# A two-block transformer kernel on Trainium2: the first pair of columns behind each norm as three float32r products

## The chip, the cores and the metric

The kernel runs on one core of one Trainium2 chip. The metric is the device time of one execution in microseconds (us); the time before is 2511.12 us, the median of 3 runs (2510.36 to 2512.72).

The core has five engines that run side by side and wait for each other through semaphores: TensorE (PE: matmuls from SBUF into PSUM), VectorE (DVE), ScalarE (ACT), GpSimd (POOL, SBUF only) and SyncE (SP, which issues the transfers here). PEld is the weight load of TensorE.

## The reference, cut to what matters

Two blocks of a network with 512 tokens and 1024 channels. The second one, where six of the seven places of the change lie, runs twice:

```python
def second_block(x, norm_g, ffn_w_gate, ffn_w_up, ffn_w_down, w_in, conv_w, pool_w, pool_scale, w_out):
    for l in range(DEPTH_2):
        g = norm_g[l]
        f = _swiglu(_rmsnorm_2(x, g[0]), ffn_w_gate[l, 0], ffn_w_up[l, 0], ffn_w_down[l, 0])
        x = x + 0.5 * _rmsnorm_2(f, g[1])
        m = _mixer(_rmsnorm_2(x, g[2]), w_in[l], conv_w[l], pool_w[l], pool_scale[l], w_out[l])
        x = x + _rmsnorm_2(m, g[3])
        f = _swiglu(_rmsnorm_2(x, g[4]), ffn_w_gate[l, 1], ffn_w_up[l, 1], ffn_w_down[l, 1])
        x = x + 0.5 * _rmsnorm_2(f, g[5])
    return x
```

`_rmsnorm_2(x, g)` is x / sqrt(mean(x²) + 1e-6) · g over the 1024 channels; `_swiglu` is silu(h @ w_gate) · (h @ w_up) @ w_down with 2816 hidden channels; `_mixer` is a projection, a stick-breaking attention over 8 heads beside a short convolution and a pooling, and a projection w_out back to 1024. The first block ends in a feed-forward part too, w_up of 1024 x 4096 behind a modulated norm of x; this norm's place is called x1 here.

## The kernel before

**Layout.** Channels lie on the 128 partitions, tokens along the free dimension: x is 8 chunks (DC = 8) of 128 x 512. A matrix product makes one *unit* of 128 output channels: for each of the 8 (or 11, in the second half of a feed-forward part) chunks of input channels one 128x128 weight tile times a 128x512 chunk, summed in one PSUM bank.

**Split products.** Almost every product is made as three float32r matmuls (L581 to L583): high part of the weights times high part of the input, high times low, low times high. The high part is a copy to float32r; the low part is what is left, full minus high. For the weights ACT makes w_hi from the loaded tile raw (`refill`, L1056) and POOL makes w_lo = raw - w_hi (L492). Weights come in *pairs* p of slots s = 0 and 1; SP loads raw for a slot when POOL has taken its low part before (lo_ready), ACT refills a slot when TensorE is through with the unit that read it (unit_done), and a unit starts when its w_lo is there (lo_ready) and its PSUM bank is free (taken).

**The first pair behind a norm.** At seven places the input of the next product has only just been made: behind x1 (L1001 to L1010) and behind norm(0) to norm(5). There the first pair of output columns is made from the *unsplit* tensors, as one float32 matmul per chunk and column: first_raw (loaded by `load_first` long ahead, in the arena's slots 12 to 15) times u_all (or u1), 16 matmuls into the two score banks (L669, L1007). After chunk 6 stands `spread`, the transposed inverse root (L638).

**Norm r**, r = 0 to 6; the last has nothing behind it. It overlaps the 8 units of the projection that come before it, the *down* units. Behind norm(0) these have 8 chunks each, behind norm(1), (3), (4) and (6) they have 11, and behind norm(2) and norm(5), which close a mixer (w_out), 8. For each output chunk c of that projection:

- DVE takes it from PSUM into f (L1982 or L1986), from norm(1) on also makes the cross product x·g·f and adds it up (L1920, L1921), and adds the two squares that ACT made to their sums (L1931, L1915).
- ACT, in this order and per slot: `refill` of the slot that the unit has freed, then f_sq and gf_sq (L1073, L1075) once DVE has taken the chunk.

Then come TensorE's token sums (L630) between thin matmuls that only keep the array busy (`keep_warm`, L625), ACT's root, DVE's reciprocal, TensorE's spread; then the update phase: DVE makes the new x chunk by chunk (L2003, L2005; in norm(0) L1989), ACT makes u_all from x (L1097) and u_hi from u_all (L1100), TensorE the first products, and when all of x is there DVE makes the 8 low parts u_lo (L1971). TensorE then goes on with the pair p+1 from u_hi and u_lo. The weights of its slot 0 are refilled between f_squares of chunk 6 and 7, those of slot 1 after chunk 1 of the update phase.

No table sets an order: each engine runs its instructions in the order written.

## Time and profile before

| | |
|---|---|
| median of 3 runs | 2511.12 us (2510.36 to 2512.72) |
| profiled execution, its own time | 2510.76 us |
| its span, first to last instruction | 2509.0 us |
| granted TensorE clock, mean | 0.997 |
| PE busy | 2477.5 us (99%) |
| DVE busy | 1283.5 us (51%) |
| ACT busy | 908.2 us (36%) |
| POOL busy | 983.5 us (39%) |
| DMA | 253 MB, mean 101 GB/s |

A matmul's record is longer than the step to the next one, since matmuls are pipelined; a busy share of 99% says that TensorE is hardly ever without work, not what the work costs. A start-to-start step does.

### The profile page before, as it was taken

What the parts mean: (1) busy time and instruction counts of PE and PEld (TensorE: products, weight loads), DVE (VectorE), ACT (ScalarE), POOL (GpSimd) and SP (SyncE); (2) the same over time, 40 slices, a digit from 0 to 9 for tenths busy, and PEclk for the clock granted to TensorE, in tenths of its full rate; (3) what the DMA queues carried; (4) which work ended last, traced back from release to release, by engine and by line L of the source; (5) the groups of instructions that cost most, each with busy time, mean ns of one, the idle gap of its engine ahead of it and who ended that gap; (6) DMA issues with size and microseconds to landing.
All of it is one profiled execution on the core that took longest, in us unless ns stands there. A gap on an engine that the chain in (4) does not pass through costs nothing.

```text
span 2509.0 us, 32788 instructions
## 1 busy us (share of the span) xinstructions
PE 2477.5 (99%) x11384; PEld 1986.7 (79%) x11384; DVE 1283.5 (51%) x1780; ACT 908.2 (36%) x1295; POOL 983.5 (39%) x445
## 2 busy tenths in 40 slices
PE   7999999999999999999999999999999999999998
PEld 4878778887788887777788887788887777788886
DVE  6664767256431358678431348431358678431334
ACT  4444543234321234454431234321234454431231
POOL 4333424443344443333343443344443333343443
PEclk9999999999999999999999999999999999999998
DMA  6222644322233231322233232233231322232232
GB/s 237 90 81 86 222 163 134 109 97 88 75 104 105 93 107 60 94 83 93 75 102 108 92 105 80 75 105 104 93 107 60 95 82 92 75 102 91 92 104 80
DMA packets 72904, 253.39 MB, mean 101 GB/s; under 512 B 9056, under 2 KB 11232, under 8 KB 72704
## 3 DMA queue, kind: packets, MB, share of 16 engines
q1 hardware_dynamic: 72832, 252.46, 30.3%
q8 instruction: 42, 0.69, 0.1%
q14 instruction: 30, 0.25, 0.0%
HBM read 244.76 MB, written 2.10 MB: 98 GB/s over the span
## 4 chain that ended last, share of the span: by engine, by line
PE 87%; issue 9%; POOL 2%; DVE 1%; DMA 1%; SPq 0%; ACT 0%; POOLq 0%; DVEq 0%; ACTq 0%
PE unit_bank L581 26%; PE unit_bank L583 26%; PE unit_bank L582 26%; PE score L669 3%; POOL w_lo L492 2%; PE mix L725 1%; PE out_bank L705 1%; PE score L1007 1%; PE mix L625 1%; PE mix L733 0%; DMA ada_in_u<-in_w_ada 0%; PE out_bank L630 0%; PE mix L630 0%; PE stat_bank L638 0%; PE score L630 0%
## 5 line engine op out<-in xcount | busy, mean ns | idle before, releaser
L492 POOL TENSOR_TENSOR w_lo<-raw,w_hi 128x1024 fp32r<-128x1024 f32 (+2 forms) x374 | 954.6, 2552 | 1483.7 <-ACT w_hi L1056 1483.7
L1056 ACT ACTIVATE w_hi<-raw 128x1024 fp32r<-128x1024 f32 (+2 forms) x375 | 415.9, 1109 | 1199.3 <-PE unit_bank L583 1177.9
L581 PE MATMUL unit_bank<-u_hi,w_hi 128*128 128x512 f32 x2152 | 845.9, 393 | 0.5 <-POOL w_lo L492 0.5
L583 PE MATMUL unit_bank<-u_hi,w_lo 128*128 128x512 f32 x2152 | 837.8, 389 | 0.0
L582 PE MATMUL unit_bank<-u_lo,w_hi 128*128 128x512 f32 x2152 | 837.7, 389 | 0.0
L581 PEld LDWEIGHTS unit_bank<-u_hi,w_hi 128*128 128x128 f32 x2152 | 403.9, 188 | 101.7 <-issue 16.0
L583 PEld LDWEIGHTS unit_bank<-u_hi,w_lo 128*128 128x128 f32 x2152 | 404.0, 188 | 84.8
L582 PEld LDWEIGHTS unit_bank<-u_lo,w_hi 128*128 128x128 f32 x2152 | 404.1, 188 | 84.2 <-issue 1.9
L581 PE MATMUL unit_bank<-h_hi,w_hi 128*128 128x512 f32 x992 | 387.0, 390 | 0.2 <-DVE h_lo L1881 0.2
L583 PE MATMUL unit_bank<-h_hi,w_lo 128*128 128x512 f32 x992 | 385.9, 389 | 0.0
L582 PE MATMUL unit_bank<-h_lo,w_hi 128*128 128x512 f32 x992 | 385.9, 389 | 0.0
L2033 DVE TENSOR_TENSOR arena<-unit_bank,rstd 128x512 f32<-128x512 f32 x84 | 58.1, 692 | 398.9 <-PE unit_bank L583 398.9
L581 PEld LDWEIGHTS unit_bank<-h_hi,w_hi 128*128 128x128 f32 x992 | 186.2, 188 | 39.5 <-DVE h_lo L1881 0.7
L582 PEld LDWEIGHTS unit_bank<-h_lo,w_hi 128*128 128x128 f32 x992 | 186.2, 188 | 39.1 <-issue 0.5
L583 PEld LDWEIGHTS unit_bank<-h_hi,w_lo 128*128 128x128 f32 x992 | 186.2, 188 | 38.9
L2042 DVE TENSOR_TENSOR h_lo<-arena,h_hi 128x512 f32 (+1 forms) x88 | 167.8, 1906 | 81.6 <-ACT h_hi L1345 81.6
L1986 DVE COPY f<-unit_bank 128x512 f32 (+1 forms) x48 | 33.2, 691 | 211.6 <-PE unit_bank L583 205.1
L2030 DVE TENSOR_TENSOR arena<-unit_bank,rstd 128x512 f32<-128x512 f32 x84 | 58.1, 692 | 121.1 <-PE unit_bank L583 121.1
L669 PE MATMUL score<-arena 128*128 128x512 f32 x192 | 85.4, 597 | 0.1
L1921 DVE TENSOR_TENSOR arena<-arena 128x512 f32<-128x512 f32 x40 | 84.2, 2105 | 1.4
L1931 DVE TENSOR_TENSOR arena<-arena 128x512 f32<-128x512 f32 x49 | 59.6, 1216 | 17.8 <-ACT arena L1073 13.5
L669 PEld LDWEIGHTS score<-arena 128*128 128x128 f32 x192 | 35.0, 190 | 42.1 <-issue 34.5
(337 smaller groups left out, 1938.0 us busy)
## 6 DMA issues: line engine op xcount, KB each, us to landing
raw<-in_w_gate_up SPq DMA_DIRECT2D x168, 512.0 KB, 3.5
raw<-in_w_down SPq DMA_DIRECT2D x64, 704.0 KB, 4.1
...
```

The source lines that it names most:

```text
L492: e.tensor_tensor(w_lo[:, s, 0:n], raw[:, s, 0:n], as32(w_hi[:, s, 0:n]), ALU.subtract).then_inc(lo_ready, 1)
L581: e.matmul(bank[:], wh, hi(k), start=n == 0, stop=False)
L582: e.matmul(bank[:], wh, lo(k), start=False, stop=False)
L583: mm = e.matmul(bank[:], wl, hi(k), start=False, stop=last)
L669: mm = e.matmul(score[s][:], first_raw[:, s, c * P:(c + 1) * P], u_all[:, c, :], start=c == 0, stop=c == DC - 1)
L1056: e.activation(w_hi[:, s, 0:n], raw[:, s, 0:n], ACT.Copy).then_inc(hi_ready, 1)
L1921: step(e.tensor_tensor(cross_acc, cross_acc, cross, ALU.add))
L1931: step(e.tensor_tensor(f_acc, f_acc, f_sq, ALU.add))
L1986: e.tensor_copy(flat(f[:, bass.ds(c, 1), :]), unit_bank[s][:]).then_inc(taken[s], 1)
L2030: g = e.tensor_tensor(ffn_g, banks[0][:], rstd[:], ALU.mult)
L2033: u = e.tensor_tensor(ffn_u, banks[1][:], rstd[:], ALU.mult)
L2042: e.tensor_tensor(flat(h_lo[:, bass.ds(i, 1), :]), ffn_h, as32(flat(h_hi[:, bass.ds(i, 1), :])), ALU.subtract).then_inc(h_ready, 1)
```

## The change

At the seven places the first pair becomes a split product too. New are first_hi (ACT, `first_high`) and first_lo (POOL, `split_first`, over first_raw in place). `first_units` on TensorE makes, per chunk c, four matmuls from u_hi (first_hi and first_lo, two columns each) and, one chunk later, two from u_lo with first_hi: 48 float32r matmuls of 128x512 in place of 16 float32 ones.

Around it:

- ACT makes u_hi straight from x and then u_all from x; the refill of slot 1 of pair p+1 moves behind all eight chunks, that of slot 0 ahead of the squares of chunk 6; first_high stands ahead of chunk 4's refill and ahead of that of slot 0 of p+1; root_u is made after chunk 3 in place of 5, and lies in PSUM.
- POOL makes u_lo of chunks 0 to 5, DVE only those of 6 and 7.
- DVE's reciprocal inv_u stands after chunk 5 in place of 7; the copy into pool_w moves behind the norm's first takes in the mixer.
- At x1 the same order holds: ACT makes u_hi and u1 from ux, POOL six low parts, DVE two.
- TensorE has one more keep_warm ahead of the first products.

SP's program is the same. The core of the diff:

```diff
@@ -153,13 +154,16 @@
         sq, x_acc, ux = slots(0, 2), slot(2), slots(4, 2)

         f_sq, gf_sq, f_acc, cross, cross_acc, gf_acc = (slot(n) for n in range(6))
-        root_f, root_u, inv_f, inv_u, scaled = (slot(11)[:, 128 + 4 * n:132 + 4 * n] for n in range(5))
+        root_f, inv_f, inv_u, scaled = (slot(11)[:, 128 + 4 * n:132 + 4 * n] for n in range(4))
         x_sum = stat[:, 0:TB]
         root_x, inv_x = stat[:, 0:TB], stat[:, TB:2 * TB]
         u1 = slots(16, 8)
         u_all = slots(16, 8)
         first_raw = arena[:, 12 * T:16 * T].rearrange("p (s n) -> p s n", s=2)
         ffn_g, ffn_s, ffn_u, ffn_h = slot(6), slot(7), slot(8), slot(9)
+
+        first_hi = nc.alloc_sbuf_tensor_at("first_hi", [P, 2, D], F32R, offset=arena_at + 6 * T * 4)
+        first_lo = nc.alloc_sbuf_tensor_at("first_lo", [P, 2, D], F32R, offset=arena_at + 12 * T * 4)
         a_pad = arena[:, 10 * T:10 * T + T + 2]
         q_st, k_st, vT_st = slot(16), slot(17), slot(18)
         v_nat = slots(19, 1)[:, 0, :].rearrange("p (i d) -> p i d", d=P)
@@ -549,15 +558,44 @@
             e.tensor_tensor(w_lo[:, 1, 0:D], raw[:, 1, 0:D], as32(w_hi[:, 1, 0:D]), ALU.subtract).then_inc(lo_ready, 1)
             split_pairs(IN1 + 2, MERGE1 - IN1 - 2, D)
             split_pairs(MERGE1, DC // 2, 6 * P)
-            split_pairs(OUT1, LAYER0 - OUT1, D)
+            def split_first(q, s):
+
+                e.wait_ge(first_hi_ready, 2 * q + s + 1)
+                e.tensor_tensor(first_lo[:, s, :], first_raw[:, s, :], as32(first_hi[:, s, :]),
+                                ALU.subtract).then_inc(first_lo_ready, 1)
+
+            def split_next(q, last, n, p):
+
+
+                if q:
+                    split_first(q, 0)
+                split_pair(last, n)
+                if q == 0:
+                    split_first(q, 0)
+                split_first(q, 1)
+                split_one(p, 0, D)
+                for c in range(DC - 2):
+                    e.wait_ge(uhi_ready, DC * (1 + q) + c + 1)
+                    e.wait_ge(u_full, DC * q + c + 1)
+                    e.tensor_tensor(u_lo[:, c, :], u_all[:, c, :], as32(u_hi[:, c, :]),
+                                    ALU.subtract).then_inc(u_ready, 1)
+                split_one(p, 1, D)
+
+            split_pairs(OUT1, DC // 2 - 1, D)
+            split_next(0, FFN1, D, FFN1 + 1)
+            split_pairs(FFN1 + 2, LAYER0 - FFN1 - 3, D)
             for l in range(LAYERS):
                 for s in range(2):
                     for half in range(2):
-                        p0, skip = ffn2(l, s, half), 1 - half
+                        p0, skip = ffn2(l, s, half), 2 - 2 * half
+                        if half == 0:
+                            split_next(FIRST_OF_NORM + 3 * l + 2 * s, p0, D if s or l == 0 else RING, p0 + 1)
                         split_pairs(p0 + skip, HALF2 - skip, D)
-                        split_pairs(p0 + HALF2, DC // 2, RING)
+                        rest = half == 0 or (l == LAYERS - 1 and s == 1)
+                        split_pairs(p0 + HALF2, DC // 2 if rest else DC // 2 - 1, RING)
                     if s == 0:
-                        split_pairs(mix2(l) + 1, MIX2_PAIRS, D)
+                        split_next(FIRST_OF_NORM + 3 * l + 1, mix2(l), RING, mix2(l) + 1)
+                        split_pairs(mix2(l) + 2, MIX2_PAIRS - 2, D)
             for n, c in enumerate(POOL_SUMS):
                 e.wait_ge(f_scaled, n + 1)
                 e.tensor_tensor(x[:, c, :], f[:, c, :], x[:, c, :], ALU.add).then_inc(x_summed, 1)
@@ -639,6 +677,30 @@
                                   start=True, stop=True)
                 mm.then_inc(spread_ready, 1)

+            def first_units(q, at=None, insert=None):
+
+
+                def low(c):
+                    e.wait_ge(u_ready, DC * (1 + q) + c + 1)
+                    for s in range(2):
+                        mm = e.matmul(score[s][:], first_hi[:, s, c * P:(c + 1) * P], u_lo[:, c, :], start=False,
+                                      stop=c == DC - 1)
+                        if c == DC - 1:
+                            mm.then_inc(first_done, 1)
+
+                e.wait_ge(first_lo_ready, 2 * q + 2)
+                for c in EIGHT:
+                    e.wait_ge(uhi_ready, DC * (1 + q) + c + 1)
+                    for w in (first_hi, first_lo):
+                        for s in range(2):
+                            e.matmul(score[s][:], w[:, s, c * P:(c + 1) * P], u_hi[:, c, :],
+                                     start=c == 0 and w is first_hi, stop=False)
+                    if c:
+                        low(c - 1)
+                    if c == at:
+                        insert()
+                low(DC - 1)
+
             def norm(r):


@@ -660,18 +722,8 @@
                 if r:
                     mm = token_sums(cross_sum, cross_acc)
                 mm.then_inc(cross_sums, 1)
-                keep_warm(3)
-                for s in range(2):
-                    e.wait_ge(first_loaded[s], 16 * (FIRST_OF_NORM + r + 1))
-                for c in EIGHT:
-                    e.wait_ge(u_full, DC * r + c + 1)
-                    for s in range(2):
-                        mm = e.matmul(score[s][:], first_raw[:, s, c * P:(c + 1) * P], u_all[:, c, :],
-                                      start=c == 0, stop=c == DC - 1)
-                        if c == DC - 1:
-                            mm.then_inc(first_done, 1)
-                    if c == 6:
-                        spread(2 * r + 2, inv_u, mix[1])
+                keep_warm(4)
+                first_units(FIRST_OF_NORM + r, 6, lambda: spread(2 * r + 2, inv_u, mix[1]))

             def u_chunk(m):
                 return lambda c: e.wait_ge(u_ready, DC * (2 + m) + c + 1)
@@ -999,15 +1051,7 @@
                               start=True, stop=True)
             mm.then_inc(x1_spread, 1)
             keep_warm(6)
-            for s in range(2):
-                e.wait_ge(first_loaded[s], 16)
-            for c in EIGHT:
-                e.wait_ge(u1_full, c + 1)
-                for s in range(2):
-                    mm = e.matmul(score[s][:], first_raw[:, s, c * P:(c + 1) * P], u1[:, c, :], start=c == 0,
-                                  stop=c == DC - 1)
-                    if c == DC - 1:
-                        mm.then_inc(first_done, 1)
+            first_units(0)
             for half in range(2):
                 p0 = FFN1 + half * FFN1_HALF
                 if half == 0:
@@ -1074,19 +1118,31 @@
                 if g is not None:
                     e.activation(gf_sq, fc, ACT.Square, scale=g(c)).then_inc(fsq_ready, 1)

+            def first_high(q, s):
+
+                e.wait_ge(first_loaded[s], 16 * (q + 1))
+                e.activation(first_hi[:, s, :], first_raw[:, s, :], ACT.Copy).then_inc(first_hi_ready, 1)
+
             def norm(r, p, part, g):


                 ahead = r < NORMS - 1
                 g = g if ahead else None
-                with e.Fori(0, DC // 2 - 1) as i:
+                def pair(i):
                     for s in range(2):
                         refill(p + i + 1, s, D if r in (2, 5) or r == 0 else RING)
                         f_squares(p + i, s, part, 2 * i + s, g)
+
+                with e.Fori(0, DC // 2 - 2) as i:
+                    pair(i)
+                if ahead:
+                    first_high(FIRST_OF_NORM + r, 0)
+                pair(DC // 2 - 2)
                 p = p + DC // 2 - 1
+                if ahead:
+                    first_high(FIRST_OF_NORM + r, 1)
+                    refill(p + 1, 0)
                 f_squares(p, 0, part, DC - 2, g)
-                if ahead:
-                    refill(p + 1, 0)
                 f_squares(p, 1, part, DC - 1, g)
                 e.wait_ge(sums_ready, r + 1)
                 token_root(root_f, square_sum)
@@ -1094,15 +1150,13 @@
                     return
                 for c in range(DC):
                     e.wait_ge(x_ready, DC * r + c + 1)
-                    e.activation(u_all[:, c, :], x[:, c, :], ACT.Identity,
-                                 scale=col("norm_g", 2 * r * DC + c)).then_inc(u_full, 1)
-                    e.wait_ge(u_full, DC * r + c + 1)
-                    e.activation(u_hi[:, c, :], u_all[:, c, :], ACT.Copy).then_inc(uhi_ready, 1)
-                    if c == 1:
-                        refill(p + 1, 1)
-                    if c == 5:
+                    gain = col("norm_g", 2 * r * DC + c)
+                    e.activation(u_hi[:, c, :], x[:, c, :], ACT.Identity, scale=gain).then_inc(uhi_ready, 1)
+                    e.activation(u_all[:, c, :], x[:, c, :], ACT.Identity, scale=gain).then_inc(u_full, 1)
+                    if c == 3:
                         e.wait_ge(grown_ready, r + 1)
                         token_root(root_u, x_sum)
+                refill(p + 1, 1)
                 e.wait_ge(spread_ready, 2 * r + 2)
                 e.activation(rstd[:], mix[1][:], ACT.Copy).then_inc(rstd_ready, 1)

@@ -1265,6 +1319,9 @@
                     if c:
                         e.wait_ge(taken[(c - 1) % 2], p0 + (c - 1) // 2 + 2)
                         square(q, c - 1)
+                    if c == refills - 1:
+                        for s in range(2):
+                            first_high(0, s)
                     if c < refills:
                         refill(p0 + c // 2 + 1, c % 2)
                 e.wait_ge(taken[1], p0 + DC // 2 + 1)
@@ -1960,14 +2016,15 @@
                             e.tensor_tensor(x_sum, x_sum, grown, ALU.add).then_inc(grown_ready, 1)
                         else:
                             e.tensor_tensor(x_sum, scaled, inv_f, ALU.mult).then_inc(grown_ready, 1)
-                    if c == DC - 1 and ahead:
+                    if c == 5 and ahead:
                         e.wait_ge(root_ready, 2 * r + 2)
                         e.reciprocal(inv_u, root_u).then_inc(inverse_ready, 1)
                 if not ahead:
                     return
-                for c in range(DC):
-
-                    e.wait_ge(uhi_ready, DC * (2 + r) + c + 1)
+                e.wait_ge(u_ready, DC * (2 + r) + DC - 2)
+                for c in range(DC - 2, DC):
+
+                    e.wait_ge(u_full, DC * (1 + r) + c + 1)
                     e.tensor_tensor(u_lo[:, c, :], u_all[:, c, :], as32(u_hi[:, c, :]),
                                     ALU.subtract).then_inc(u_ready, 1)
                 e.wait_ge(rstd_ready, r + 1)
```

Norm(2), the place between the mixer's w_out and the feed-forward part, on POOL. w_lo, raw and w_hi are the weights' low part, full tile and high part, hi_ready ACT's word that w_hi is there. Before, one turn of the loop over pairs, which runs on through the norm:

```order
L492 TENSOR_TENSOR w_lo<-raw,w_hi 128x1024 [waits hi_ready]
L491 REGISTER_ALU
L492 TENSOR_TENSOR w_lo<-raw,w_hi 128x1024 [waits hi_ready]
L496 REGISTER_ALU
L496 COMPARE_AND_BRANCH
```

Now, from the end of that loop's turns on:

```order
L497 TENSOR_TENSOR w_lo<-raw,w_hi 128x1024 [waits hi_ready]
L505 REGISTER_ALU
L505 COMPARE_AND_BRANCH
L564 TENSOR_TENSOR first_lo<-arena,first_hi 128x1024 [waits first_hi_ready]
L497 TENSOR_TENSOR w_lo<-raw,w_hi 128x1024 [waits hi_ready] x2
L564 TENSOR_TENSOR first_lo<-arena,first_hi 128x1024 [waits first_hi_ready]
L497 TENSOR_TENSOR w_lo<-raw,w_hi 128x1024 [waits hi_ready]
L580 TENSOR_TENSOR u_lo<-arena,u_hi 128x512 [waits u_full,uhi_ready] x6
L497 TENSOR_TENSOR w_lo<-raw,w_hi 128x1024 [waits hi_ready]
```

Two splits of the first pair have come in around the splits for the last two down units, and six of u_lo stand between slot 0 and slot 1 of the next pair.

The same norm on ACT. Before, from the end of the loop over chunks 0 to 5:

```order
L1073 ACTIVATE arena<-f 128x512 [waits consts_loaded,cols_loaded,taken0]
L1075 ACTIVATE arena<-f,cols 128x512
L1056 ACTIVATE w_hi<-raw 128x1024 [waits raw_loaded0,unit_done]
L1073 ACTIVATE arena<-f 128x512 [waits consts_loaded,cols_loaded,taken1]
L1075 ACTIVATE arena<-f,cols 128x512
L1066 ACTIVATE arena<-out_bank,eps 128x4 [waits sums_ready]
L1097 ACTIVATE arena<-x,cols 128x512 [waits x_ready]
L1100 ACTIVATE u_hi<-arena 128x512 [waits u_full]
```

Now, from the end of the loop over chunks 0 to 3:

```order
L1124 ACTIVATE first_hi<-arena 128x1024 [waits first_loaded0]
L1100 ACTIVATE w_hi<-raw 128x1024 [waits raw_loaded0,unit_done]
L1117 ACTIVATE arena<-f 128x512 [waits consts_loaded,cols_loaded,taken0]
L1119 ACTIVATE arena<-f,cols 128x512
L1100 ACTIVATE w_hi<-raw 128x1024 [waits raw_loaded1,unit_done]
L1117 ACTIVATE arena<-f 128x512 [waits consts_loaded,cols_loaded,taken1]
L1119 ACTIVATE arena<-f,cols 128x512
L1124 ACTIVATE first_hi<-arena 128x1024 [waits first_loaded1]
L1100 ACTIVATE w_hi<-raw 128x1024 [waits raw_loaded0,unit_done]
L1117 ACTIVATE arena<-f 128x512 [waits consts_loaded,cols_loaded,taken0]
L1119 ACTIVATE arena<-f,cols 128x512
```

Two copies to first_hi have come in, and the refill of slot 0 of the next pair stands ahead of the squares of chunk 6.

## Rows read from the trace of the kernel before

**Rows 1.** The page: engines' busy time, and the chain that ended last.

```profile
PE 2477.5 (99%) x11384; PEld 1986.7 (79%) x11384; DVE 1283.5 (51%) x1780; ACT 908.2 (36%) x1295; POOL 983.5 (39%) x445
...
PE 87%; issue 9%; POOL 2%; DVE 1%; DMA 1%; SPq 0%; ACT 0%; POOLq 0%; DVEq 0%; ACTq 0%
```

**Rows 2.** TensorE by time, x1 and norm(0): start, duration, instruction, count.

```profile
346.21 13.97 PE L1007 MATMUL score<-arena 128*128 128x512 f32 x32 [0.40 <-ACT arena L1283]
...
618.80 12.26 PE L669 MATMUL score<-arena 128*128 128x512 f32 x28
630.89 1.05 PE L638 MATMUL mix<-tabs,arena 128*128 128x128 f32 x8
...
633.74 0.40 PE L582 MATMUL unit_bank<-u_lo,w_hi 128*128 128x512 f32 x1
...
634.21 0.39 PE L581 MATMUL unit_bank<-u_hi,w_hi 128*128 128x512 f32 x1
...
634.90 0.39 PE L581 MATMUL unit_bank<-u_hi,w_hi 128*128 128x512 f32 x1
```

**Rows 3.** Groups by line and shape: count, busy us, mean ns of one.

```profile
L492 POOL TENSOR_TENSOR w_lo<-raw,w_hi 128x1024 fp32r<-128x1024 f32 x302 | 732.0, 2424 | 1213.0 <-ACT w_hi L1056 1213.0
...
L563 POOL TENSOR_TENSOR x<-f,x 128x512 f32<-128x512 f32 x4 | 5.0, 1266 | 16.4 <-DVE f L2000 16.4
...
L1056 ACT ACTIVATE w_hi<-raw 128x1024 fp32r<-128x1024 f32 x303 | 320.7, 1059 | 875.6 <-PE unit_bank L583 855.7 <-DMA raw<-in_w_in 9.3 <-DMA raw<-in_w_out 6.9
...
L1097 ACT ACTIVATE arena<-x,cols 128x512 f32<-128x512 f32 x48 | 34.3, 715 | 18.3 <-DVE x L2005 16.0 <-DVE x L1989 2.2
```

**Rows 4.** By time, norm(1)'s update phase: DVE, POOL, TensorE.

```profile
986.99 0.69 DVE L2005 TENSOR_TENSOR x<-unit_bank,x 128x512 f32<-128x512 f32 x1
...
992.43 0.75 DVE L2003 SCALAR_TENSOR_TENSOR unit_bank<-f,half_g,stat_bank 128x512 f32<-128x512 f32 x1
...
993.82 0.74 DVE L2003 SCALAR_TENSOR_TENSOR unit_bank<-f,half_g,stat_bank 128x512 f32<-128x512 f32 x1
...
998.07 4.87 DVE L1971 TENSOR_TENSOR u_lo<-arena,u_hi 128x512 fp32r<-128x512 f32 x8
...
991.51 2.37 POOL L492 TENSOR_TENSOR w_lo<-raw,w_hi 128x1024 fp32r<-128x1024 f32 x1 [11.16 <-ACT w_hi L1056]
...
1001.67 1.88 PE L669 MATMUL score<-arena 128*128 128x512 f32 x4
```

**Rows 5.** By time, down units ahead of norm(2): POOL, DVE, TensorE.

```profile
1172.57 2.40 POOL L492 TENSOR_TENSOR w_lo<-raw,w_hi 128x1024 fp32r<-128x1024 f32 x1 [3.04 <-ACT w_hi L1056]
1181.33 2.87 POOL L492 TENSOR_TENSOR w_lo<-raw,w_hi 128x1024 fp32r<-128x1024 f32 x1 [6.36 <-ACT w_hi L1056]
...
1167.78 0.69 DVE L1986 COPY f<-unit_bank 128x512 f32 x1 [0.75 <-DVE arena L1915]
...
1172.94 0.69 DVE L1986 COPY f<-unit_bank 128x512 f32 x1 [0.45 <-DVE arena L1915]
1173.79 1.72 DVE L1920 SCALAR_TENSOR_TENSOR arena<-x,cols,f 128x512 f32 x1 [0.16 <-DVE f L1986]
...
1178.32 0.69 DVE L1986 COPY f<-unit_bank 128x512 f32<-128x512 f32 x1 [0.41 <-DVE arena L1915]
...
1182.23 0.69 DVE L1986 COPY f<-unit_bank 128x512 f32<-128x512 f32 x1 [0.26 <-PE unit_bank L583]
1182.96 1.78 DVE L1920 SCALAR_TENSOR_TENSOR arena<-x,cols,f 128x512 f32<-128x512 f32 x1
...
1182.09 1.05 PE L630 MATMUL out_bank<-tabs,arena 128*128 128x1 f32 x8
```

**Rows 6.** By time, DVE in the down units ahead of norm(1).

```profile
968.71 3.60 DVE L1921 TENSOR_TENSOR arena<-arena 128x512 f32<-128x512 f32 x1
...
974.43 0.69 DVE L1982 TENSOR_TENSOR f<-unit_bank,f 128x512 f32<-128x512 f32 x1 [0.45 <-PE unit_bank L583]
```

**Rows 7.** By time, TensorE in norm(6).

```profile
2492.66 0.39 PE L583 MATMUL unit_bank<-h_hi,w_lo 128*128 128x512 f32 x1
...
2496.16 2.08 PE L638 MATMUL stat_bank<-tabs,arena 128*128 128x128 f32 x8 [0.57 <-DVE arena L1945]
```

**Rows 8.** Stretches: us, busy (count) per engine, granted clock, DMA share, GB/s.

```profile
2495.50:2496.00 0.50, 0.10 (x1) 0.01 (x1) 0.07 (x1) 0.26 (x1) 0.00 (x0) 0.50 0.00 0
```

38 lines of the change are left out of this document (21 added, 17 removed).

## The prediction

> **What bounds the kernel now.** I read the page first: TensorE is busy for 99% of the span, and the chain that ended last runs through it for 87% [rows 1]. So a change counts by what it does to the time at which TensorE gets from one piece of work to the next. Then TensorE by time at the seven places. The reader should see a step, not a duration: in a split unit the next float32r matmul starts 0.23 us after the last (0.69 us for three, 24 of them in 5.44) [rows 2]. At norm(0) the first pair holds TensorE from 618.80 to 633.5, one step before 633.74: 14.7 us, of which 0.9 are the spread, so 13.8 for 16 products, 0.86 each. At x1 it is the same 13.8 [rows 2]. Three steps are 0.68, so the split product as such is the cheaper one: 48 x 0.227 = 10.9 us, 2.9 less per place, if its operands are there in time.
>
> Then DVE and POOL by time, ahead of norm(2), since the change gives both of them and ACT more to do there. Two things are to be seen. First, DVE takes a chunk at 1167.78, 1172.94 and 1178.32, every 5.2 to 5.4 us, and a down unit there lasts 5.44: DVE has nothing to spare. Second, instructions of DVE with two SBUF operands stand still while POOL runs: the cross product took 1.72 us at 1173.79, as POOL's split ran from 1172.57 to 1174.97, and 1.78 at 1182.96, under the split that began at 1181.33 [rows 5]; one with an operand in PSUM isn't held: 0.75 at 992.43, inside POOL's 991.51 to 993.88 [rows 4]. POOL is held by DVE the same way: 2.87 us at 1181.33 against a mean of 2.42 [rows 3, 5].
>
> **x1 and norm(0): a gain.** Added on the path: 48 steps, 10.9 us; removed 13.8. ACT now needs 2 x 0.61 us (0.715 long, the next starts 0.1 before its end) per chunk for u_hi and u_all [rows 3], TensorE 6 x 0.227 = 1.36, so after a wait of 0.15 to 0.3 us at chunk 1 TensorE sets the pace. u_lo by POOL costs 1.27 each by the row of the same shape [rows 3], one per 1.36, and is used a chunk later; DVE's two come before TensorE asks for them. The extra keep_warm adds 0.1 at norm(0). The new splits of the weights (2 x 1.06 on ACT, 2 x 2.42 on POOL) lie under the units ahead, where ACT and POOL wait for TensorE; without that cover they would cost up to 2.4 each. Gain 2.6 each (bounds 2.0 and 2.9).
>
> **Update phase of norm(1) to norm(5).** There DVE sets the pace: a chunk of x every 1.39 us (992.43 to 993.82), and four small sums after chunk 3 [rows 4], so x7 is there 10.7 us after x0. TensorE then still has, from u_hi of chunk 6 on, 4 + 2 products, the spread of 0.9, and 4 + 4 products: 4.1 us. From x0 to the next unit that makes 14.25 us, where before it was 15.7 (x0 there at 987.68, the last four float32 passes from 1001.67 on, 0.43 each) [rows 4]. The gain is 1.4, not 2.9. The late refill of slot 1 costs nothing: split 3.5 us after x7, the unit that wants it starts 8 us after x7. The 4.87 us of eight low parts on DVE [rows 4] lay under the first products before; now six move to POOL.
>
> Here a page speaks against the change. The Trainium skill, Perfetto Trace Analysis, "Optimizing Scalar/DVE Operations", says that GpSimd and DVE share a read port, so that moving work between the two might not help. If that held in the update phase, each of six low parts would stop a DVE instruction for up to 1.27 us, 7.6 per norm, and the total would be 30 us and more above the sum below. The row at 992.43 shows 0.75 us beside a running split, and the skill's own finer rule (SBUF — State Buffer, "Who interferes with whom": a DVE instruction with at most one SBUF input is left alone, one with two contends) agrees with the trace. I take no cost in the update phase.
>
> **Down units ahead of norm(2) and norm(5): a loss.** Per unit of 5.44 us, POOL's split (2.40) and DVE's four sums and products on SBUF (3 x 0.69 + 0.75, 2.8) exclude each other: 5.2, beside the 0.69 of the take that may overlap. The pair is full, as the takes' dates show [rows 5]. The change puts three more splits into the stretch from chunk 3 to the sums of chunk 6: the two of first_raw (2.40 each) and that of pair p+1, slot 0, which came at 1181.33, when chunk 6 was all but through, and now comes before. That is 7.2 us with room for almost none. I laid the instructions end to end in each engine's order, each with its duration and gap of rows like these and each waiting for what it waits for; for the kernel before this puts TensorE's sums at 1182.1 and the spread at 1185.6, where the trace has 1182.09 [rows 5] and 1185.74. For the kernel after it gives: chunk 4 taken at 1171.6 instead of 1167.8; ACT, which stands at that chunk's squares, refills for unit 7 only after it; chunk 5 taken at 1178.0 instead of 1172.9, so that units 6 and 7, which want these PSUM banks, wait 1 us each (2.1 in all); chunk 6's last sum at 1189.0 instead of 1182.0, which TensorE's first token sum waits for. So TensorE idles from 1184.2 to 1189.0. Chunk 7's cross product is no longer held (-1.0 less overlap, -0.25), and the update phase gives 1.4 back: 6.9 - 0.25 - 1.4 = +5.3 per norm, 10.6 for both. No row shows who goes first when both wait at POOL's end; with DVE first it is 5.3, with POOL first up to 6.5. Below, nothing under 3 follows unless DVE is faster than its rows.
>
> **Down units ahead of norm(1), (3), (4): a wash.** A unit lasts 7.48 us, POOL's split 3.25, DVE is through with chunk 5 just as unit 6 ends (held 3.60 us at 968.71, next take 974.43 with 0.45 idle) [rows 6]. Laid out alike, the two extra splits and the earlier one put chunk 6's last sum 0.9 us behind the end of unit 7. 0.9 - 1.4 = -0.5 each (bounds -1.4 and +0.9), -1.5 for three.
>
> **The clock.** With nearly 5 us idle ahead of the thin sums of norm(2) and (5) I expect the granted clock to fall there. The row for it is norm(6): last wide product at 2492.66, thin matmuls and less than 1 us idle after it, and at 2495.50 the clock stood at 0.50 [rows 7, 8], the 1.2 GHz level; the spread took 2.08 us [rows 7] against 1.05 [rows 2]. Between nothing and all five thin groups at half speed (4.4) I take 1.5 per norm, nearest to the spread's 1.0: 3.0.
>
> **Sum**, against the profiled run's own 2510.76 (span 2509.0, 1.8 around it; the median, 2511.12, is 0.4 above): -2.6 - 2.6 - 1.5 + 10.6 + 3.0 = +6.9. On the median: 2518.0.
>
> The pool_w copy (0.9 us of DVE, twice) moves to where DVE next waits for ACT; it may be held by one split, 2.4 us, and TensorE asks for that work some 4 us later: nothing. DMA: the same transfers; first_raw lands long before ACT reads it.
>
> **Rivals.**
> - *No queue builds up* (the other side: faster). If the splits of the first pair fall into gaps of DVE, TensorE never waits in the down units: -2.6 - 2.6 - 5 x 1.4 = -12.2, 2498.9. It decides by one date: whether chunk 6's last sum ends before unit 7. For it: POOL is idle for 61% of the span. Against: the takes' spacing. Chance 0.15.
> - *The queue, but the clock holds*: +3.9, 2515.0. The idle stretch may be shorter, and keep_warm stands behind it. 0.23.
> - *The clock stays low into the products*: 5 instead of 1.5 per norm, +13.9, 2525.0. For it: 1.36 us of products per chunk become 2.7, above DVE's 1.39. 0.12.
> - *The split product isn't cheaper here*: if the change of bank and weights at each matmul costs 0.06 us a step, the 48 take what the 16 took; x1 and norm(0) give nothing: +12.1, 2523.2. Against: three weights per three steps are changed in a unit as well [rows 2]. 0.05.
>
> **Chances.** The forecast has 0.45, with its own range of 2514 to 2527 (the bounds above, POOL first included). About 0.2% of the time, 5.0 us, is what a measurement can tell from no change; 2506.1 to 2516.1 is "same". Faster 0.16 (the first rival and a hair), same 0.27 (the second, and the forecast's low end), slower 0.57. The range, 2509 to 2527, leaves out the first rival and the far ends.
>
> **What would show it.** Right: in norm(2) and (5) a gap on TensorE between the last down unit and the first token sum of 3 to 6 us, ended by DVE's last sum of chunk 6; DVE's additions there at 2.4 us and more instead of 0.69; POOL back to back around two first_lo; a granted clock under 1 at the sums. At x1 and norm(0) about 11 us instead of 13.8 for the first pair. Wrong: sums that start as the last unit ends, at all places; or DVE's x chunks further apart than 1.4 us while POOL makes u_lo, which would refute the reading of rows 4.

## The result: 17.8 us slower, and the profile after

The changed kernel takes 2529.45 us (median of 6 runs, 2523.73 to 2533.87), the kernel before 2511.67 us (6 runs): ratio 1.0071, 95% interval 1.0061 to 1.0081. The forecast was 2518.0 us with a range of 2509 to 2527. The sign was right; the size was not, and the time lies outside the range. The profiled run took 2531.15 us, its span is 2529.4. The lines that answer [rows 1] are these, from the page and its list of cores:

```profile
PE 2483.4 (98%) x11508; PEld 2027.8 (80%) x11508; DVE 1289.5 (51%) x1738; ACT 923.3 (37%) x1309; POOL 1075.8 (43%) x501
...
PE 78%; issue 9%; DVE 9%; POOL 2%; DMA 1%; DVEq 0%; ACT 0%; SPq 0%; POOLq 0%; ACTq 0%
...
core 0: 2529.4 us, clock 0.988
```

In the chain that ended last DVE has gone from 1% to 9% and TensorE from 87% to 78%: more of the time that decides the end now passes in waits of TensorE for DVE. The mean granted clock was 0.997 before.

**x1 and norm(0)**, TensorE by time (answers [rows 2]; L696 are the products with u_hi, L686 those with u_lo, L619 and L620 open the next unit):

```profile
346.27 0.70 PE L696 MATMUL score<-u_hi,first_hi 128*128 128x512 f32 x2 [0.41 <-ACT u_hi L1341]
...
357.52 0.39 PE L619 MATMUL unit_bank<-u_hi,w_hi 128*128 128x512 f32 x1
357.75 0.39 PE L620 MATMUL unit_bank<-u_lo,w_hi 128*128 128x512 f32 x1
...
616.30 0.70 PE L696 MATMUL score<-u_hi,first_hi 128*128 128x512 f32 x2
...
628.51 0.39 PE L619 MATMUL unit_bank<-u_hi,w_hi 128*128 128x512 f32 x1
```

The first pair takes 11.25 us at x1, and all that follows comes 2.5 us earlier than before, 5.0 us after norm(0).

**Down units ahead of norm(2)**, POOL, then DVE, then TensorE by time (answers [rows 5]; all dates here lie 5.82 us ahead of those before, the gain so far; L497 splits a unit's weights, L564 first_raw, L2043 takes a chunk, L1971 is its last sum):

```profile
1159.33 2.46 POOL L564 TENSOR_TENSOR first_lo<-arena,first_hi 128x1024 fp32r<-128x1024 f32 x1 [1.07 <-ACT first_hi L1124]
1161.77 2.84 POOL L497 TENSOR_TENSOR w_lo<-raw,w_hi 128x1024 fp32r<-128x1024 f32 x1
1169.00 2.41 POOL L497 TENSOR_TENSOR w_lo<-raw,w_hi 128x1024 fp32r<-128x1024 f32 x1 [4.40 <-ACT w_hi L1100]
1175.42 2.41 POOL L564 TENSOR_TENSOR first_lo<-arena,first_hi 128x1024 fp32r<-128x1024 f32 x1 [4.00 <-ACT first_hi L1124]
1177.79 2.80 POOL L497 TENSOR_TENSOR w_lo<-raw,w_hi 128x1024 fp32r<-128x1024 f32 x1
...
1159.67 2.68 DVE L1987 TENSOR_TENSOR arena<-arena 128x512 f32<-128x512 f32 x1
1162.50 2.65 DVE L1971 TENSOR_TENSOR arena<-arena 128x512 f32<-128x512 f32 x1
1166.00 0.69 DVE L2043 COPY f<-unit_bank 128x512 f32 x1 [0.85 <-PE unit_bank L621]
...
1169.32 2.65 DVE L1971 TENSOR_TENSOR arena<-arena 128x512 f32<-128x512 f32 x1 [0.16 <-DVE arena L1987]
1172.42 0.69 DVE L2043 COPY f<-unit_bank 128x512 f32 x1 [0.45 <-DVE arena L1971]
...
1175.72 2.65 DVE L1971 TENSOR_TENSOR arena<-arena 128x512 f32<-128x512 f32 x1
...
1182.63 0.69 DVE L1971 TENSOR_TENSOR arena<-arena 128x512 f32<-128x512 f32 x1
...
1166.75 0.50 PE L619 MATMUL unit_bank<-h_hi,w_hi 128*128 128x512 f32 x1 [1.26 <-DVE f L2043]
...
1173.26 0.47 PE L619 MATMUL unit_bank<-h_hi,w_hi 128*128 128x512 f32 x1 [0.77 <-DVE f L2043]
...
1183.43 1.86 PE L668 MATMUL out_bank<-tabs,arena 128*128 128x1 f32 x8 [4.49 <-DVEq L1990]
```

Each time one of the splits of POOL above runs beside it, an addition of DVE with two operands in SBUF takes 2.65 us instead of 0.69. So two units start late, and TensorE idles for 4.5 us ahead of the first token sum. That sum itself then takes 1.86 us where it took 1.05 at 1182.09 [rows 5].

**Update phase of norm(1)**: the groups' row of POOL's low parts of u, then DVE and POOL by time (answers [rows 3, 4]; L2060 begins the update of a chunk of x):

```profile
L580 POOL TENSOR_TENSOR u_lo<-arena,u_hi 128x512 fp32r<-128x512 f32 x42 | 53.9, 1293 | 88.9 <-ACT arena L1155 78.8
...
991.10 0.72 DVE L2060 SCALAR_TENSOR_TENSOR unit_bank<-f,half_g,stat_bank 128x512 f32<-128x512 f32 x1
...
992.46 0.75 DVE L2060 SCALAR_TENSOR_TENSOR unit_bank<-f,half_g,stat_bank 128x512 f32<-128x512 f32 x1
...
984.99 5.45 POOL L580 TENSOR_TENSOR u_lo<-arena,u_hi 128x512 fp32r<-128x512 f32 x4 [12.06 <-ACT arena L1155]
991.22 2.69 POOL L580 TENSOR_TENSOR u_lo<-arena,u_hi 128x512 fp32r<-128x512 f32 x2 [0.78 <-ACT arena L1155]
```

A low part costs POOL 1.29 us (1.27 forecast), and beside two of them DVE's updates come every 1.36 to 1.39 us, not later than before.

**The granted clock**, from the table by stretch (columns: stretch, length, busy us and count of PE, PEld, DVE, ACT, POOL, granted clock, DMA share, GB/s): norm(2), norm(3), norm(4).

```profile
1189.00:1196.00 7.00, 7.00 (x35) 7.00 (x35) 4.82 (x8) 2.86 (x5) 1.38 (x2) 0.50 0.00 0
...
1561.00:1569.00 8.00, 8.00 (x42) 8.00 (x43) 5.40 (x10) 3.21 (x6) 1.46 (x2) 0.55 0.00 0
...
1935.00:1940.00 5.00, 5.00 (x38) 5.00 (x36) 2.94 (x5) 0.95 (x2) 0.00 (x0) 0.77 0.00 0
```

0.50 is the 1.2 GHz level; the other two stretches are in part at it. In the kernel before, the same stretches of all five norms have 1.00.

**Where the 20.4 us of the two spans are.** I took four dates at every place (last matmul of the last unit, first token sum, first product, next unit) from both traces and put down, step by step, how much later each comes after the change, in us:

| term | forecast | measured |
|---|---|---|
| x1, norm(0) | -2.6 -2.6 | -2.49 -2.55 |
| queue at norm(2), norm(5): units late and sums late | +6.9 +6.9 | +7.16 +7.26 |
| sums late at norm(1), (3), (4) | 3 x 0.9 | +0.88 +0.87 +1.01 |
| from the first product on, five norms | 5 x -1.4, 2 x -0.25 | -1.63 -1.20 -1.62 -1.62 -1.18 = -7.25 |
| behind the sums of norm(6): the clock falls later there (spread 1.62 us, before 2.08) | 0 | -0.5 |
| thin matmuls between first sum and first product, norm(1) to (5): the clock | 3.0 | 0 +5.60 +3.37 +1.47 +5.60 = +16.04 |
| sum | +6.8 (6.9 as rounded there) | +20.4 |

Every term but one is within 0.5 us of its forecast. The clock is off by 13 us. It also takes 1.0 us in the row of the first products, at norm(2), norm(3) and norm(5): without the fall the part from the first product on would have given 8.2 us.

### The profile page after: what moved, and what is told of

The parts are those of the page before. It is cut to its first block, busy times and chain, and to the rows that moved or that the text cites. A ratio compares the mean times of both kernels' runs of the same rounds, so it can differ in the third digit from the quotient of the medians.

```text
span 2529.4 us, 33006 instructions
## 1 busy us (share of the span) xinstructions
PE 2483.4 (98%) x11508; PEld 2027.8 (80%) x11508; DVE 1289.5 (51%) x1738; ACT 923.3 (37%) x1309; POOL 1075.8 (43%) x501
## 4 chain that ended last, share of the span: by engine, by line
PE 78%; issue 9%; DVE 9%; POOL 2%; DMA 1%; DVEq 0%; ACT 0%; SPq 0%; POOLq 0%; ACTq 0%
PE unit_bank L619 23%; PE unit_bank L620 23%; PE unit_bank L621 23%; DVE arena L1977 2%; PE score L696 2%; POOL w_lo L497 2%; DVE arena L1971 2%; DVE arena L1976 1%; DVE arena L1987 1%; PE score L686 1%; PE mix L663 1%; PE mix L777 1%; PE out_bank L757 1%; PE out_bank L668 1%; PE mix L785 0%
## 5 line engine op out<-in xcount | busy, mean ns | idle before, releaser
L497 POOL TENSOR_TENSOR w_lo<-raw,w_hi 128x1024 fp32r<-128x1024 f32 (+2 forms) x374 | 956.1, 2557 | 1313.3 <-ACT w_hi L1100 1313.2
L619 PE MATMUL unit_bank<-u_hi,w_hi 128*128 128x512 f32 x2152 | 843.0, 392 | 0.4 <-POOL w_lo L497 0.4
L620 PE MATMUL unit_bank<-u_lo,w_hi 128*128 128x512 f32 x2152 | 837.7, 389 | 0.0
L619 PEld LDWEIGHTS unit_bank<-u_hi,w_hi 128*128 128x128 f32 x2152 | 403.9, 188 | 100.4 <-issue 14.3
L620 PEld LDWEIGHTS unit_bank<-u_lo,w_hi 128*128 128x128 f32 x2152 | 404.0, 188 | 82.6 <-issue 0.2
L619 PE MATMUL unit_bank<-h_hi,w_hi 128*128 128x512 f32 x992 | 387.4, 391 | 4.3 <-DVE f L2043 4.0
L620 PE MATMUL unit_bank<-h_lo,w_hi 128*128 128x512 f32 x992 | 386.0, 389 | 0.0
L619 PEld LDWEIGHTS unit_bank<-h_hi,w_hi 128*128 128x128 f32 x992 | 186.2, 188 | 45.3 <-DVE f L2043 3.4
L620 PEld LDWEIGHTS unit_bank<-h_lo,w_hi 128*128 128x128 f32 x992 | 186.2, 188 | 38.8 <-issue 0.5
L2043 DVE COPY f<-unit_bank 128x512 f32 (+1 forms) x48 | 33.2, 692 | 212.0 <-PE unit_bank L621 206.2
L580 POOL TENSOR_TENSOR u_lo<-arena,u_hi 128x512 fp32r<-128x512 f32 x42 | 53.9, 1293 | 88.9 <-ACT arena L1155 78.8
L1400 ACT ACTIVATE h_hi<-arena 128x512 f32 (+1 forms) x88 | 55.6, 632 | 34.0 <-DVE arena L2097 33.5
## 6 DMA issues: line engine op xcount, KB each, us to landing
ada_in_u<-in_w_ada SPq DMA_DIRECT2D x8, 512.0 KB, 11.3
```

The lines of the kernel that those rows point to most:

```text
L497: e.tensor_tensor(w_lo[:, s, 0:n], raw[:, s, 0:n], as32(w_hi[:, s, 0:n]), ALU.subtract).then_inc(lo_ready, 1)
L580: e.tensor_tensor(u_lo[:, c, :], u_all[:, c, :], as32(u_hi[:, c, :]), ALU.subtract).then_inc(u_ready, 1)
L619: e.matmul(bank[:], wh, hi(k), start=n == 0, stop=False)
L620: e.matmul(bank[:], wh, lo(k), start=False, stop=False)
L1400: e.activation(h_hi[:, bass.ds(i, 1), :].rearrange("p a t -> p (a t)"), ffn_h, ACT.Copy).then_inc(hhi_ready, 1)
```

## Experiments

Each run is told by its distance to the kernel before on the same chip (median 2512.2, 2511.5 or 2510.5 us in the three sets; 13 to 25 runs each). The changed kernel stands at +17.8, from 6 runs of each kernel. One such distance is sure to 2.5 us with ten runs and to 4 us with four (the intervals of the ratios); a difference of two of them is less sure still.

### Is it the clock? a_fill

```diff
+                for _ in range({1: 4, 2: 21, 3: 4, 4: 4, 5: 21}.get(r, 0)):
+                    e.matmul(mix[1][:], u_hi[:, 0, 0:P], u_hi[:, 0, :], start=True, stop=True)
                 e.wait_ge(fsq_added, (DC - 1) * (r + 1))
```

> The changed kernel with TensorE kept at work in the gap ahead of the token sums: 21 wide matmuls of 0.227 us (4.8 us) at norm(2) and norm(5), 4 (0.9 us) at norm(1), (3) and (4), their result unused. The waits of DVE, POOL and the two units of 1.26 and 0.77 us stay. Theory 'the granted clock falls because TensorE stood idle': the thin sums run at full clock (1.05 instead of 1.86 us for the first), the 5.6 + 3.4 + 1.5 + 5.6 = 16.1 us of slow thin matmuls go, 2529.5 - 16 = 2513.5 us, mean clock 0.997 instead of 0.988. Rival 'the clock falls for another reason (the date, the thin matmuls themselves)': 2529 us, first sum of norm(2) still 1.86 us.

2512.92 us (10 runs, 2512.50 to 2514.76), +0.7, ratio 1.0006 (0.9996 to 1.0016). TensorE by time and the table by stretch at norm(2):

```profile
1177.80 4.92 PE L709 MATMUL mix<-u_hi 128*128 128x512 f32 x21
1182.56 0.99 PE L668 MATMUL out_bank<-tabs,arena 128*128 128x1 f32 x8
...
1189.34 0.71 PE L696 MATMUL score<-u_hi,first_hi 128*128 128x512 f32 x2
...
1182.50:1189.30 6.80, 6.80 (x60) 6.75 (x60) 5.18 (x9) 2.35 (x5) 0.00 (x0) 1.00 0.02 7
```

The sum starts as late as in the changed kernel (4.99 us behind the last unit), but from it to the first product it is now 6.8 us, at all five norms, where it was 12.8 at norm(2) and norm(5), 10.2 at norm(3) and 8.4 at norm(4). Work whose result nobody reads gives back 17 us, and the scatter of 10 us between runs has gone with it. So with the idle stretch filled the clock holds, and the lowered clock is most of the loss: what the late units and sums cost (17.2 us in the table) and what the products gain (13.3) leave 4 us by the dates and 0.7 by the medians.

### Is it the queue of DVE and POOL? b_nolow and e_order

In b_nolow POOL only passes the semaphore on at norm(2) and norm(5), and the low products read first_hi:

```diff
                 e.wait_ge(first_hi_ready, 2 * q + s + 1)
+                if q in (FIRST_OF_NORM + 2, FIRST_OF_NORM + 5):
+                    e.sem_inc(first_lo_ready, 1)
+                    return
```

> The changed kernel without the two splits of first_lo on GpSimd at norm(2) and norm(5); the low products there take first_hi in place of first_lo, so part of the computation is left out; TensorE's instructions, ACT's first_hi and all orders stay. Theory 'these splits fill the DVE and GpSimd pair': the waits of units 6 and 7 (1.26 and 0.77 us) go, the idle stretch ahead of the sums shrinks from 4.9 us to 1 or less, the clock mostly holds there: 2 x (about 6 of the queue + 3 to 5.6 of the clock) less, 2506 to 2512 us. Rival 'it is ACT's first_hi and the refill of slot 0, which now comes ahead of the squares of chunk 6': 2527 to 2530 us, the gap stays over 3 us.

2510.02 us (10 runs), -2.2, ratio 0.9993 (0.9983 to 1.0003). The waits of units 6 and 7 are gone, and the first sum of norm(2) comes 1.36 us behind the last unit instead of 4.87:

```profile
1178.82 1.05 PE L671 MATMUL out_bank<-tabs,arena 128*128 128x1 f32 x8 [0.98 <-DVEq L1994]
```

That is 6.1 us less at each of the two norms, 12.2 of the 20.0 us between the two kernels; the clock did the rest, though it did not hold everywhere (0.80 in the sums of norm(1) and (2), 0.60 in those of norm(5)). The other 1.1 us of gap must then be the third split, which e_order moves back:

```diff
                 if ahead:
                     first_high(FIRST_OF_NORM + r, 1)
+                    if r == 0:
+                        refill(p + 1, 0)
+                f_squares(p, 0, part, DC - 2, g)
+                if ahead and r:
                     refill(p + 1, 0)
-                f_squares(p, 0, part, DC - 2, g)
```

> The changed kernel with ACT's refill of slot 0 for the pair behind the norm put back behind the squares of chunk 6 at norm(1) to (5); so that pair's low split on GpSimd comes behind DVE's last sum again, as before the change; the two splits of first_lo stay. Theory 'three splits in the queue of DVE and GpSimd, this being the third': about 2.4 of the 4.6 us of idle ahead of the sums go at norm(2) and (5), and the 0.9 us at norm(1), (3), (4) may go with it: 5 to 7 us of waits less, a little of the clock with it, 2516 to 2525 us. Rival 'the place of this split costs nothing, the two of first_lo are all of it': 2527 to 2531 us, gap still 4.5 us.

2517.75 us (9 runs), +6.2, ratio 1.0029 (1.0018 to 1.0039). Inside the range of the first theory, but not by its sizes: at norm(2) the idle stretch went only from 4.49 to 3.58 us, not by 2.4, while at norm(1), (3) and (4) the sum now starts 0.23 us behind the last unit, as before. At norm(2):

```profile
1181.15 1.87 PE L668 MATMUL out_bank<-tabs,arena 128*128 128x1 f32 x8 [3.58 <-DVEq L1993]
```

The trace of the changed kernel says why: the split at 1177.79 (above) ran beside DVE's take of chunk 6 and held only the cross product behind it, by 0.9 us. In sum 4.6 us of waits went; the other 7 are the clock. The queue at norm(2) and (5) is the two splits of first_lo, the gap at the other three is the place of one refill.

### How much idle time does the clock bear? c_gap, f_gap2, i_fill134

Both kernels are the kernel before with one wait more on TensorE at norm(1) to (5): until DVE has taken chunk 7 (c_gap), or until ACT has squared it (f_gap2).

```diff
+                if p_last is not None and r < NORMS - 1:
+                    e.wait_ge(taken[1], p_last + 2)
                 e.wait_ge(fsq_added, (DC - 1) * (r + 1))
```

> The kernel before with one wait more: at norm(1) to norm(5) TensorE starts its first token sum only when DVE has taken chunk 7, about 1 us after the last unit; nothing else changed. Theory 'an idle gap of about 1 us there is enough for the granted clock to fall at some norms, as at norm(3) and (4) of the changed kernel': 5 x 0.9 = 4.5 us of wait and 1.5 to 3.5 us of slow thin matmuls at two to four norms, 2519 to 2527 us, clock 0.994 or less. Rival 'the clock fell at norm(3) and (4) for something else that the change brings': 2511.7 + 4.5 = 2516 us, clock 0.997.

2521.45 us (10 runs, 2514.97 to 2527.68), +9.3, ratio 1.0039 (1.0028 to 1.0051). The sums start 0.94 us later at norm(1), (3) and (4) and 0.89 at norm(2) and (5). At these two TensorE waited for DVE behind the sums already in the kernel before, and 0.4 us of that is saved, so the waits cost 3.7 us in all; the other 5.6 are the clock. In the profiled run it fell at norm(3) and norm(4), not at (1), (2), (5), though the gap was the same at all five. TensorE at norm(3):

```profile
1556.16 1.05 PE L630 MATMUL out_bank<-tabs,arena 128*128 128x1 f32 x8 [0.79 <-DVE f L1984]
1557.07 0.91 PE L625 MATMUL mix<-tabs 128*128 128x128 f32 x6
1557.83 1.15 PE L630 MATMUL out_bank<-tabs,arena 128*128 128x1 f32 x8
1558.84 1.63 PE L625 MATMUL mix<-tabs 128*128 128x128 f32 x6
```

The thin matmuls start at full clock (0.91 us for six) and are at 1.63 from 1558.84 on. With the longer wait:

> The kernel before with the first token sum of norm(1) to (5) waiting for ACT's squares of chunk 7, so a gap of about 1.9 us instead of none; the run with the gap of 0.94 us gave 2521.5 us, 4.7 of it waits and 4.6 the clock. Theory 'the longer TensorE stands idle, the more often the clock falls': 5 x 1.7 = 8.5 us of waits and 8 to 20 us of slow thin matmuls, 2529 to 2540 us. Rival 'how long the gap is makes no difference, each of them costs 0.9 us on the mean': 2511.7 + 8.5 + 4.6 = 2525 us.

2534.22 us (4 runs), +22.7, ratio 1.0092 (1.0075 to 1.0109): 7.0 us of waits (1.6 each, less what they save behind the sums) and 15.7 of the clock. And the changed kernel with only its short gaps filled, at norm(1), (3), (4):

> The changed kernel with the four wide matmuls ahead of the token sums at norm(1), (3) and (4) only; norm(2) and (5) keep their idle stretch of 4.6 us. Theory 'the long idle stretch costs 5.6 us of clock each time, the short one of 1.1 us some 1.5 us on the mean': 2529.5 - 3 x 1.6 = 2524.5 us (2522 to 2527), with a smaller scatter than 2523.7 to 2533.9. Rival 'the short ones cost nothing on the mean (the profiled run was an unlucky one)': 2529 us. Rival 'they make most of it': 2518 us or less.

2522.19 us (4 runs), +11.7, ratio 1.0045 (1.0028 to 1.0061). So the three short gaps cost 6.1 us of clock (17.8 - 11.7) and the two long ones 11.0 (11.7 - 0.7). Per gap, what the clock costs on the mean, against the kernel before; the last column is my estimate of how sure that is, from the intervals of the ratios:

| kernel | idle ahead of the sums, us | clock, us per norm | from, to |
|---|---|---|---|
| c_gap | 0.9 | 5.6 / 5 = 1.1 | 0.7, 1.8 |
| changed, norm(1), (3), (4) | 0.9 | 6.1 / 3 = 2.0 | 0.4, 3.6 |
| f_gap2 | 1.6 | 15.7 / 5 = 3.1 | 2.4, 4.1 |
| changed, norm(2), (5) | 4.7 | 11.0 / 2 = 5.5 | 3.1, 7.9 |

So a longer wait costs more clock (the first row against the third); the two rows with 0.9 us do not differ beyond what such runs can tell.

### Does any work hold the clock? j_thin

a_fill with `keep_warm({1: 6, 2: 31, 3: 6, 4: 6, 5: 31}.get(r, 0))` in place of the wide matmuls.

> The changed kernel with the gap ahead of the token sums filled by thin matmuls (128x128 float32, as keep_warm makes them, six in 0.91 us): 31 at norm(2) and (5), 6 at norm(1), (3), (4). Theory 'any work on TensorE holds the granted clock, as keep_warm does between the sums of the kernel before': as with wide ones, 2513 us, clock 0.997. Rival 'thin matmuls are too little for it once there are 11 us of them instead of 7': 2518 to 2530 us, the clock at 0.50 in the sums of norm(2) and (5).

2517.09 us (10 runs, 2515.66 to 2519.00), +6.6, ratio 1.0025 (1.0015 to 1.0034), mean clock 0.998. The clock stands at 1.00 through 14 us of thin matmuls in the profiled run. My filling was too long: six records in 0.91 us are three matmuls, so 31 took this long at norm(2):

```profile
1177.82 7.08 PE L663 MATMUL mix<-tabs 128*128 128x128 f32 x62
1184.73 0.95 PE L668 MATMUL out_bank<-tabs,arena 128*128 128x1 f32 x8
```

The sum comes 2.2 us later than in a_fill, twice, and 0.4 us later at the other three: 5.5 of the 5.9 us between the two. So thin work in the gap does what wide work does. That the gap is the only thing that lowers the clock doesn't follow: see h_two and d_late.

### The gains by themselves: h_two and g_dve

h_two splits the first pair at x1 and norm(0) only; norm(1) to (5) are as in the kernel before.

> Only the x1 and norm(0) parts of the change; norm(1) to (5) as in the kernel before, with the float32 first pair. Theory 'each of the two places gives 2.5 us and carries nothing into the rest': 2512.0 - 5.0 = 2507 us, clock 0.997. Rival 'the gain at x1 and norm(0) is lost further on (the date of the norms against the clock or the loads)': 2510 to 2512 us.

2505.79 us (10 runs), -5.7, ratio 0.9977 (0.9968 to 0.9987): the 5.2 forecast, to within what a run can tell.

Its trace has something else. At norm(5) the first sum comes 0.29 us behind the last unit (2116.33), as in the kernel before, with no gap; all the same the granted clock is at 0.50 from about 2123.2 to 2126.6:

```profile
2116.62 1.05 PE L672 MATMUL out_bank<-tabs,arena 128*128 128x1 f32 x8
...
2122.97 1.39 PE L667 MATMUL mix<-tabs 128*128 128x128 f32 x6
2124.16 13.43 PE L736 MATMUL score<-arena 128*128 128x512 f32 x28
```

The six fills take 1.39 us instead of 0.91, and this norm 1.4 us more than in the kernel before. So the thin stretch can lose its clock without a wait ahead of it, later and for less.

g_dve is the kernel d_late of the next section with all low parts of u at norm(1) to (5) made by DVE, and the products that read them at the end:

```diff
-                for c in range(DC - 2):
+                for c in range(DC - 2 if q <= FIRST_OF_NORM else 0):
                     e.wait_ge(uhi_ready, DC * (1 + q) + c + 1)
```

> The version with the late first_lo (2498.7 us), but at norm(1) to (5) DVE makes all eight low parts of u after its updates of x and GpSimd none; TensorE takes the products with u_lo last. Theory 'GpSimd's u_lo beside the updates of DVE is free, and is worth what DVE would need at the end': the eight of 0.61 us stand behind x7, 2.5 us per norm, 2498.7 + 12 = 2511 us (2507 to 2515). Rival 'GpSimd's low parts hold DVE as much as they save it': 2499 to 2503 us.

2516.54 us (10 runs), +5.0, ratio 1.0020 (1.0010 to 1.0030), so 18 us above d_late where I expected 12 (2511, at most 2515). From the first sum to the next unit at norm(3) it takes 24.0 us, in d_late 20.5, in the kernel before 21.7 (with the 0.4 us by which that unit's first step is longer there). The low parts by POOL, with the order of products that they allow, are worth 3.5 us per norm, and without them the split products are slower there than the float32 ones.

### The repair: d_late

POOL splits first_raw only after DVE's last sum (cross_ready), ahead of the low parts of u, where DVE's updates all have an operand in PSUM. TensorE takes the products with first_lo and u_lo one or two chunks later. ACT's refill goes back as in e_order.

```diff
+                    split_one(p, 0, D)
+                    e.wait_ge(cross_ready, q)
                     split_first(q, 0)
-                split_first(q, 1)
-                split_one(p, 0, D)
+                    split_first(q, 1)
...
+                    for step_of in ("h0", "h1", "w", "l0", "l1", "h2", "u0", "l2", "h3", "u1", "l3", "h4", "u2", "l4",
+                                    "h5", "u3", "l5", "h6", "u4", "l6", "s", "u5", "h7", "l7", "u6", "u7"):
```

(h, l, u: the products of a chunk with first_hi, first_lo, u_lo; w: the wait for first_lo; s: the spread.)

> The changed kernel with the low parts of the first pair split later at norm(1) to (5): GpSimd does them after DVE's last sum of gain times squares (cross_ready), in the update phase, ahead of the low parts of u; TensorE takes products with first_lo and u_lo one or two chunks later than those with first_hi; ACT's refill of slot 0 is behind the squares of chunk 6 again. Theory 'the loss was the queue of DVE and GpSimd and the clock behind it': sums start as the last unit ends, the clock holds, x1 and norm(0) give 2.5 each and the five norms 1.6 each, 2511.7 - 5.0 - 8.0 = 2498.7 us. Rival 'GpSimd's splits now hold DVE in the update phase or come late for TensorE': up to 4.8 us per norm more, 2499 to 2523 us, with waits on first_lo or u_lo in front of products. If the clock falls all the same: 3 to 6 us more per norm.

2498.65 us (4 runs, 2497.91 to 2499.44), -13.5, ratio 0.9945 (0.9928 to 0.9961), mean clock 0.997. It is faster than both kernels. That the median meets the 2498.7 expected is partly luck: by the dates the five norms give 1.1 us each and not 1.6, and the two profiled runs are 11.3 us apart. POOL, DVE and TensorE at norm(2):

```profile
1180.84 4.69 POOL L564 TENSOR_TENSOR first_lo<-arena,first_hi 128x1024 fp32r<-128x1024 f32 x2 [2.21 <-DVEq L2031]
1185.47 7.80 POOL L586 TENSOR_TENSOR u_lo<-arena,u_hi 128x512 fp32r<-128x512 f32 x6
...
1181.37 0.75 DVE L2087 SCALAR_TENSOR_TENSOR unit_bank<-f,cols,stat_bank 128x512 f32<-128x512 f32 x1 [0.67 <-PE stat_bank L682]
...
1182.77 0.74 DVE L2087 SCALAR_TENSOR_TENSOR unit_bank<-f,cols,stat_bank 128x512 f32<-128x512 f32 x1
...
1184.16 0.74 DVE L2087 SCALAR_TENSOR_TENSOR unit_bank<-f,cols,stat_bank 128x512 f32<-128x512 f32 x1
...
1176.55 1.03 PE L674 MATMUL out_bank<-tabs,arena 128*128 128x1 f32 x8
```

The same two splits that took DVE's additions to 2.65 us leave its updates at 0.75 and a chunk of x every 1.39 us. The last unit's last matmul is at 1176.32, the first sum 0.23 us behind it. The stretch from the first product to the next unit is 13.7 us at norm(1), against 13.2 in a_fill: in the new order TensorE wants chunk 1 right behind chunk 0 and stands idle for 0.57 us.

Here too the clock fell once without a gap, at norm(2), to 0.50 from about 1183.2 to 1186.6. Norm(2), then norm(5), by stretch:

```profile
1176.00:1184.00 8.00, 7.81 (x62) 7.34 (x61) 6.82 (x10) 2.62 (x5) 5.79 (x3) 0.95 0.21 68
1184.00:1198.00 14.00, 14.00 (x63) 11.47 (x62) 10.91 (x21) 12.44 (x19) 11.43 (x8) 0.91 0.00 0
...
2113.00:2121.00 8.00, 7.80 (x64) 7.33 (x64) 6.83 (x10) 2.66 (x5) 5.80 (x3) 1.00 0.19 68
```

It cost nothing: from the first sum to the next unit both norms take 20.88 us; the 0.57 us that TensorE stands idle behind the first chunk at norm(5) are filled at norm(2).

## Why the prediction was wrong, and where it was right

- **x1 and norm(0)**: forecast -2.6 each, measured -2.5 each in the traces and -5.7 for both in h_two. Right. One reading was off without harm: the next unit begins at 633.10, not 633.5, and 0.4 of the 13.8 us put down to the products are the longer first step of that unit (last section).
- **The queue in the down units**: forecast, in dates of the kernel before, chunk 4 taken at 1171.6, chunk 5 at 1178.0, first sum at 1189.0. Measured, with the 5.82 us added: 1171.8, 1178.2, 1189.25. TensorE stood idle for 1.26 and 0.77 us ahead of units 6 and 7, forecast 1 each. Right, and b_nolow shows that the first_lo splits are its cause. The forecast counted three equal splits (7.2 us with room for almost none); the third is worth only 0.9 us there (e_order), the two of first_lo 6.1.
- **Norm(1), (3), (4)**: sums forecast 0.9 us late, 0.9 to 1.0 measured. Right as far as it went: I put the gap into the sum and did not ask what it does to the clock.
- **The update phase**: from the first product on -7.25 us, forecast -7.5. So near is partly luck: the products gave 1.6 us per norm instead of 1.4, and the fallen clock took 1.0 back. DVE's chunks came 1.39 us apart beside POOL's u_lo, so the reading of [rows 4] held, and the rule of the Trainium skill that stood beside it (SBUF — State Buffer, "Who interferes with whom": a DVE instruction with at most one SBUF input is left alone, one with two contends) agrees with the trace on both sides: 0.75 us in the updates, 2.65 in the additions. The page of the Trainium skill that spoke against the change (Perfetto Trace Analysis, "Optimizing Scalar/DVE Operations": moving work between GpSimd and DVE might not help) says only "might", and in this phase the move did help: g_dve is 3.5 us per norm slower without it.
- **The clock: the step that failed.** "Between nothing and all five thin groups at half speed (4.4) I take 1.5 per norm", for norm(2) and (5) alone, 3.0 in all. In the profiled run it was 16.0 (17.0 with the first products); by the fill it is 17.1 on the mean, within some 3.5 us. It has three faults. The middle of two bounds was no reading: the one place for it [rows 7, 8] has the clock at 0.50 and the spread at 2.08 us 3.5 us behind the last wide product, with less than 1 us idle, which speaks for the upper end. That end was too low itself, since the keep_warm matmuls run at the lower clock as well: 6.8 us became 12.8, 6 and not 4.4. And norm(1), (3), (4) got nothing, although 0.9 us idle was forecast for them and norm(6) had lost its clock behind 0.66 us idle between its two sums.
- **Of the rivals**, the third (clock low into the products, +13.9) comes nearest. The first products of norm(2) do run at 0.50, until 1199.81, but only 0.4 us is lost by it. Its size was near (5 us per norm at two of them), but for another reason: norm(2) lost 6.0 us in the thin matmuls ahead of the products.

What stays open: why the clock falls behind some gaps of 0.9 us and not behind equal ones (norm(1) of the changed kernel kept it, norm(3) not), and now and then with no gap ahead of the sums (norm(5) of h_two, norm(2) of d_late; both have 0.2 to 0.3 us idle behind the second sum, as norm(2) and (5) of the kernel before have, whose profiled run kept the clock). The runs of the kernel before spread over 4 to 6 us too, the longer ones mostly with the lower mean clock (0.996 against 0.998). The runs give means only; whether gaps of 0.9 us cost more in the changed kernel (2.0 us) than in c_gap (1.1) they can't tell.
